# Delta rule and Hyena convolution on one core: scaled keys from ScalarE inside the inversion, a last level that updates one matrix, no barrier behind it, and the convolution's copies first

## What is computed

```python
a = jnp.where(strict, jnp.einsum('nbhid,nbhjd->nbhij', kb, kc) * decay, 0.0)
t_inv = lax.linalg.triangular_solve(eye + a, jnp.broadcast_to(eye, a.shape), left_side=True, lower=True)
u = t_inv @ (vc * bc[..., None])
w = t_inv @ (kb * jnp.exp(gc)[..., None])
k_dec = kc * jnp.exp(gc[..., -1:] - gc)[..., None]
...
v_new = u_i - jnp.einsum('bhck,bhkv->bhcv', w_i, state)
state = state * ge_i[..., None, None] + jnp.einsum('bhck,bhcv->bhkv', kd_i, v_new)
```

## Time and profile before

| | us |
|---|---|
| median of 3 runs | 2621.1 (2616.09, 2621.1, 2623.4) |
| the profiled execution | 2617.3 |
| its span | 2615.5 |
| PE busy | 2498.7 (96%) |
| DVE busy | 1501.8 (57%) |
| ACT busy | 938.6 (36%) |
| POOL busy | 835.9 (32%) |
| granted clock of PE, mean | 0.972 |

### The profile page before, as it was taken

How to read it: one execution, slowest core, us unless ns; L and a number is a source line. 1 busy time by engine, 2 the same in 40 slices (tenths; PEclk the granted TensorE clock), 3 DMA queues, 4 the chain that set the end, 5 groups by cost and what they waited for, 6 DMA issues and landing times.

```text
span 2615.5 us, 37266 instructions
## 1 busy us (share of the span) xinstructions
PE 2498.7 (96%) x14492; PEld 2053.0 (78%) x14492; DVE 1501.8 (57%) x2134; ACT 938.6 (36%) x1419; POOL 835.9 (32%) x446
## 2 busy tenths in 40 slices
PE   7899899999999989998999999999998999999998
PEld 5667887888888877866788888888886766788887
DVE  5766745635755878487555456654675477524242
ACT  4366213322223646336433222122255432433231
POOL 3433002454442222224223322322223331354443
PEclk9999888999997999999999999999998999999999
DMA  5412001444441110212013333422321020232222
GB/s 210 170 50 89 3 7 59 172 134 159 163 153 57 49 49 1 63 57 35 18 48 127 99 113 128 137 91 94 121 73 55 30 84 33 81 113 97 97 97 80
DMA packets 78567, 228.49 MB, mean 87 GB/s; under 512 B 21456, under 2 KB 23504, under 8 KB 77786
## 3 DMA queue, kind: packets, MB, share of 16 engines
q1 hardware_dynamic: 66216, 181.31, 20.9%
q10 hardware_dynamic: 12210, 45.20, 5.2%
HBM read 224.37 MB, written 2.12 MB: 87 GB/s over the span
## 4 chain that ended last, share of the span: by engine, by line
PE 83%; DVE 8%; ACT 4%; issue 4%; POOL 1%; DMA 1%; DVEq 0%; ACTq 0%; POOLq 0%; SPq 0%
PE ps L271 21%; PE ps L272 21%; PE ps L273 21%; PE ps L769 3%; PE ps L784 2%; PE ps L800 2%; PE ps L440 1%; PE ps L392 1%; POOL w_lo L2472 1%; DVE rstd L681 1%; PE ps L350 1%; PE ps L351 1%; PE ps L352 1%; DVE small L861 1%; PE ps L449 1%
## 5 line engine op out<-in xcount | busy, mean ns | idle before, releaser
L2472 POOL TENSOR_TENSOR w_lo<-ring,w_hi 128x1024 fp32r<-128x1024 f32 x292 | 711.5, 2437 | 1353.5 <-ACT w_hi L264 850.0
L271 PE MATMUL ps<-act_hi,w_hi 128*128 128x512 f32 x2280 | 840.9, 369 | 7.6 <-DVE mix_lo L957 6.0
L273 PE MATMUL ps<-act_hi,w_lo 128*128 128x512 f32 x2280 | 827.8, 363 | 0.0
L272 PE MATMUL ps<-act_lo_ffn,w_hi 128*128 128x512 f32 (+1 forms) x1408 | 512.9, 364 | 0.0
L271 PEld LDWEIGHTS ps<-act_hi,w_hi 128*128 128x128 f32 x2280 | 428.8, 188 | 91.1 <-issue 15.8
L273 PEld LDWEIGHTS ps<-act_hi,w_lo 128*128 128x128 f32 x2280 | 427.8, 188 | 71.5
L264 ACT CAST w_hi<-ring 128x1024 fp32r<-128x1024 f32 (+1 forms) x167 | 173.5, 1040 | 698.6 <-PE ps L273 610.8
L1150 ACT CAST w_hi<-ring 128x1024 fp32r<-128x1024 f32 (+1 forms) x132 | 137.5, 1043 | 460.9 <-PE ps L273 460.9
L272 PEld LDWEIGHTS ps<-act_lo_ffn,w_hi 128*128 128x128 f32 x1408 | 265.1, 188 | 42.2 <-issue 0.7
L1070 DVE SCALAR_TENSOR_TENSOR ada_place<-ada_place 128x1024 f32<-128x1024 f32 x164 | 252.4, 1539 | 23.6 <-DMA ada_place<-in_w_ada 9.8
L271 PE MATMUL ps<-hidden_hi,w_hi 128*128 128x512 f32 x704 | 256.3, 364 | 1.8 <-DVE hidden_lo L1231 1.5
(11 more groups left out here) (371 smaller groups left out, 3368.7 us busy)
## 6 DMA issues: line engine op xcount, KB each, us to landing
ring<-in_w_ffn SPq DMA_DIRECT2D x204, 512.0 KB, 3.3
ada_place<-in_w_ada ACTq DMA_DIRECT2D x82, 512.0 KB, 4.3
ring<-in_w_gdn SPq DMA_DIRECT2D x16, 512.0 KB, 3.3
mix<-in_w_ada SPq DMA_DIRECT2D x14, 512.0 KB, 3.5
ring<-in_w_hy SPq DMA_DIRECT2D x12, 512.0 KB, 3.3
ring<-in_w_dil_qk SPq DMA_DIRECT2D x8, 512.0 KB, 8.2
ring<-in_w_out SPq DMA_DIRECT2D x8, 512.0 KB, 3.2
ring<-in_w_diff_qk SPq DMA_DIRECT2D x8, 512.0 KB, 3.3
```

The source lines that it names most:

```text
L271: pe.matmul(out, w[0], x[0], start=start, stop=False)
L272: pe.matmul(out, w[0], x[1], start=False, stop=False)
L273: return pe.matmul(out, w[1], x[0], start=False, stop=stop)
L2472: pool.tensor_tensor(k.w_lo[:, a % SPLITS, :], k.ring[:, a % SLOTS, :], k.w_hi[:, a % SPLITS, :].bitcast(F32), ALU.subtract).then_inc(k.lo ...
```

## The change

- The scaled keys `kbe` and `k_tok` are made by ScalarE, in 32 ACTIVATEs of 128x128 that stand behind the copies of levels 0 to 3 of the inversion (one head per level).
- The last level leaves out the products and updates of `t`.
- The barrier behind the inversion is gone; the u products of a head wait for that head's `inv_updated`, the w products for `apply_kbe`.
- Apply's blocks are ordered u, u, w, w for two heads at a time. VectorE clears the state before it copies w.
- `keep_warm` at the end of apply is one matmul, not four.
- In Hyena, ScalarE's and VectorE's barrier behind the projection is gone, and all four `skipped` multiplications stand behind the copies of the bins and of z.

The diff, without the list of stages and with one of the engines' barrier lines for each of the two stages:

```diff
--- before.py
+++ after.py
@@ -1964,7 +1964,8 @@
         for h in range(GH):
             blk = slice(4 * h, 4 * h + 4)
             v.eng.wait_ge(k.sem("inv_z"), GH * lev + h + 1)
-            link(v, v.eng.tensor_tensor(m["t"][:, blk, :], m["t"][:, blk, :], small_bank(k, 4 + h), ALU.subtract))
+            if lev < LEVELS - 2:
+                link(v, v.eng.tensor_tensor(m["t"][:, blk, :], m["t"][:, blk, :], small_bank(k, 4 + h), ALU.subtract))
             v.eng.tensor_tensor(m["tt"][:, blk, :], m["tt"][:, blk, :], small_bank(k, h), ALU.subtract).then_inc(k.sem("inv_updated"), 1)
             v.eng.wait_ge(k.sem("inv_updated"), GH * lev + h + 1)
 
@@ -1989,33 +1990,44 @@
             for b in range(PAIRS):
                 i = 4 * h + b
                 for r in HALVES:
-                    pe.matmul(small_bank(k, 4 + h, r)[:, b, :], m["tt"][r, i, :], m["a"][r, i, :], start=True, stop=True)
+                    if lev < LEVELS - 2:
+                        pe.matmul(small_bank(k, 4 + h, r)[:, b, :], m["tt"][r, i, :], m["a"][r, i, :], start=True, stop=True)
                     last = pe.matmul(small_bank(k, h, r)[:, b, :], m["a"][r, i, :], m["tt"][r, i, :], start=True, stop=True)
             last.then_inc(k.sem("inv_z"), 1)
 
 
 def gdn_invert_scalar(k, s):
     m = gdn_views(k)
+
+    def keys(h):
+        for b in range(PAIRS):
+            i, at = 4 * h + b, GH * b + h
+            s.eng.activation(m["kbe"][:, i, :], m["k_tok"][:, i, :], ACT.Copy, scale=k.small[:, 80 + at:81 + at])\
+                .then_inc(k.sem("apply_kbe"), 1)
+        s.eng.wait_ge(k.sem("apply_kbe"), PAIRS * (h + 1))
+        for b in range(PAIRS):
+            i, at = 4 * h + b, GH * b + h
+            s.eng.activation(m["k_tok"][:, i, :], m["k_tok"][:, i, :], ACT.Copy, scale=k.small[:, 64 + at:65 + at])\
+                .then_inc(k.sem("apply_keys"), 1)
+
     for lev in range(LEVELS - 1):
         for h in range(GH):
             s.eng.wait_ge(k.sem("inv_x"), GH * lev + h + 1)
             s.eng.copy(m["a"][:, 4 * h:4 * h + 4, :], small_bank(k, h)).then_inc(k.sem("inv_x_kept"), 1)
             s.eng.wait_ge(k.sem("inv_x_kept"), GH * lev + h + 1)
+        if lev < GH:
+            keys(lev)
 
 
 def gdn_apply_vector(k, v):
     m = gdn_views(k)
     for h in range(GH):
-        blk = slice(4 * h, 4 * h + 4)
-        v.eng.tensor_tensor(m["kbe"][:, blk, :], m["k_tok"][:, blk, :], spread(by_head(k, 80)[:, h, :], P), ALU.mult).then_inc(k.sem("apply_kbe"), 1)
-        v.eng.wait_ge(k.sem("apply_kbe"), h + 1)
-        link(v, v.eng.tensor_tensor(m["k_tok"][:, blk, :], m["k_tok"][:, blk, :], spread(by_head(k, 64)[:, h, :], P), ALU.mult))
         link(v, v.eng.tensor_tensor(m["qkvg"][:, h, :], m["qkvg"][:, h, :], m["egc"][:, h, :], ALU.mult))
+    link(v, v.eng.memset(m["state"], 0.0))
     for n in range(2):
-        v.eng.wait_ge(k.sem("apply_made"), 2 * n + 2)
+        v.eng.wait_ge(k.sem("apply_turned"), n + 1)
         for e, r in enumerate(HALVES):
             link(v, v.eng.tensor_copy(m["wt"][:, 8 * n:8 * n + 8, r], k.bank(4 + 2 * n + e).rearrange("p (b n) -> p b n", b=8)))
-    link(v, v.eng.memset(m["state"], 0.0))
 
 
 def gdn_apply_scalar(k, s):
@@ -2024,25 +2036,31 @@
         s.eng.wait_ge(k.sem("apply_made"), h + 1)
         s.eng.copy(m["u"][:, 4 * h:4 * h + 4, :], k.bank(h).rearrange("p (b n) -> p b n", b=4)).then_inc(k.sem("apply_kept"), 1)
     s.eng.wait_ge(k.sem("apply_kept"), GH)
+    s.eng.wait_ge(k.sem("apply_keys"), GH * PAIRS)
 
 
 def gdn_apply_tensor(k, pe):
 
     m = gdn_views(k)
-    for h in range(GH):
-        pe.wait_ge(k.sem("apply_kbe"), h + 1)
-        for b in range(PAIRS):
-            i = 4 * h + b
-            for e, r in enumerate(HALVES):
-                pe.matmul(k.ps[r, h * 512 + b * P:h * 512 + (b + 1) * P], m["tt"][r, i, :], m["v_tok"][r, i, :], start=True, stop=True)
-        for b in range(PAIRS):
-            i = 4 * h + b
-            for e, r in enumerate(HALVES):
-                last = pe.matmul(k.bank(4 + 2 * (h // 2) + e, CHUNK, (i % 8) * CHUNK), m["kbe"][r, i, :], m["tt"][r, i, :],
-                                 start=True, stop=True)
-        last.then_inc(k.sem("apply_made"), 1)
+    for n in range(2):
+        for h in (2 * n, 2 * n + 1):
+            pe.wait_ge(k.sem("inv_updated"), GH * (LEVELS - 2) + h + 1)
+            for b in range(PAIRS):
+                i = 4 * h + b
+                for e, r in enumerate(HALVES):
+                    last = pe.matmul(k.ps[r, h * 512 + b * P:h * 512 + (b + 1) * P], m["tt"][r, i, :], m["v_tok"][r, i, :],
+                                     start=True, stop=True)
+            last.then_inc(k.sem("apply_made"), 1)
+        for h in (2 * n, 2 * n + 1):
+            pe.wait_ge(k.sem("apply_kbe"), PAIRS * (h + 1))
+            for b in range(PAIRS):
+                i = 4 * h + b
+                for e, r in enumerate(HALVES):
+                    last = pe.matmul(k.bank(4 + 2 * n + e, CHUNK, (i % 8) * CHUNK), m["kbe"][r, i, :], m["tt"][r, i, :],
+                                     start=True, stop=True)
+        last.then_inc(k.sem("apply_turned"), 1)
     pe.wait_ge(k.sem("apply_kept"), 1)
-    keep_warm(k, pe, 0, 4)
+    keep_warm(k, pe, 0, 1)
 
 
 def gdn_scan_tensor(k, pe):
@@ -2313,9 +2331,6 @@
         link(s, s.eng.copy(k.sq[:, 0, 0:S], k.bank(bank(0))))
         s.eng.copy(k.sq[:, 1, 0:S], k.bank(bank(2))).then_inc(k.sem(done), 1)
 
-    s.eng.wait_ge(k.sem("hy_taps_made"), 4)
-    for c in range(3):
-        skipped(c)
     s.eng.wait_ge(k.sem("hy_kernel_bins"), 1)
     s.eng.wait_ge(k.sem("hy_summed"), 1)
     left(0, odd_banks, "hy_kernel_left")
@@ -2324,7 +2339,9 @@
         s.eng.wait_ge(k.sem("hy_z_turned"), c + 1)
         s.eng.copy(b["z"][:, :, c * P:(c + 1) * P], k.bank(turned_bank(c)).rearrange("p (t n) -> p t n", t=4))\
             .then_inc(k.sem("hy_z_kept"), 1)
-    skipped(3)
+    s.eng.wait_ge(k.sem("hy_taps_made"), 4)
+    for c in range(4):
+        skipped(c)
     s.eng.wait_ge(k.sem("hy_bins"), 1)
     s.eng.wait_ge(k.sem("hy_kernel_kept"), 1)
     left(0, even_banks, "hy_bins_left")
@@ -2549,7 +2566,6 @@
     gdn_products_tensor(k, pe)
     k.after(pe, "gdn_products")
     gdn_invert_tensor(k, pe)
-    k.after(pe, "gdn_invert")
     gdn_apply_tensor(k, pe)
     k.after(pe, "gdn_apply")
     gdn_scan_tensor(k, pe)
@@ -2656,7 +2671,6 @@
     k.pairs["gqa"].scalar(s)
     end("gqa_attend")
     hy_project_scalar(k, s)
-    end("hy_project")
     hy_inverse_scalar(k, s)
     end("hy_inverse")
     along_scalar(k, s, "w_out_o", k.sem("mix_o_evac"), "mod_f1", k.x, S)
```

More of the change, by code:

```diff
@@ L79 @@
     "start", "norm1", "dil_project", "dil_attend", "gdn_project", "gdn_masks",
-    "gdn_products", "gdn_invert", "gdn_apply", "gdn_scan", "gdn_out", "mix1_split", "mix1_out", "mix1_post", "norm2",
+    "gdn_products", "gdn_apply", "gdn_scan", "gdn_out", "mix1_split", "mix1_out", "mix1_post", "norm2",
     "ffn1", "ffn1_post",
@@ L83 @@
     "mix_e_split", "mix_e_out", "mod_f0", "ffn2",
-    "mod_a1", "gqa_project", "gqa_attend", "hy_project", "hy_inverse", "mix_o_out", "mod_f1", "ffn3", "end",
+    "mod_a1", "gqa_project", "gqa_attend", "hy_inverse", "mix_o_out", "mod_f1", "ffn3", "end",
 ]
@@ L2614, in scalar_program @@
     gdn_invert_scalar(k, s)
-    end("gdn_invert")
     gdn_apply_scalar(k, s)
```

## The result

The changed kernel takes 2598.88 us (median of 4 runs, 2594.7 to 2601.37), the kernel before 2622.25 us (4 runs). The ratio is 0.9913, with a 95% interval of 0.9891 to 0.9935: 17 to 29 us less. The profiled execution has a span of 2596.8 us, 18.7 us less than before.

The account below looks back on a forecast made before the run. The prediction took TensorE, 83% of the chain that ended last, to bound the kernel. Gains of 1.89 + 2.05 + 7.6 + 4.45 = 16.0 us (delta rule) and 4.7 (Hyena), 20.7 together, from 2619.2 gave 2598.5 us, range 2591 to 2607.

Parts of the forecast that it names:

- Last level: Inversion's last level: half of the 128 second products go, taking 1.89 us from TensorE's path.
- No idle before apply: Between inversion and apply: u products wait only for their head's update, so TensorE's 2.05 us of idle go.
- ScalarE's keys: Inversion's first four levels: eight added ACTIVATEs each, 3.2 to 3.4 us, fit ScalarE's 3.86 us idle and cost nothing.
- seven of the eight multiplications: VectorE's lost key multiplications in apply: only the first was on the path, the other seven ran beside TensorE, worth nothing.
- Clock in apply: Apply: with no idle ahead the clock stays 1.00, so 15.2 us become 7.6, a gain of 7.6 us.
- the first rival: Apply's w products do not follow the clock: 2.9 us less gain, 2601.4 us; chance 0.08 together with late keys.
- End of apply: Last w block to scan: one warm matmul, VectorE's last copies decide, 1.85 us in place of 6.3, gain 4.45 us.
- Hyena: Hyena part: ScalarE's bins copy goes first, 3.3 us; shorter TensorE idle keeps the clock, 1.4 us more.
- The sum: Whole kernel: 16.0 us in the delta rule and 4.7 in Hyena, 20.7 us gained.
- The slower rival: Scan starts at half clock and never recovers: its 32 us become up to 64, total 2630 or 2638; chance 0.05.

Follow-up runs that it names:

- e11: The changed kernel with the barrier behind the inversion put back: 2600.61 us, ratio 0.9921.
- e7: The changed kernel with the scaled keys made by VectorE inside apply, no barrier: seven executions, one of 2604.24 us, six from 2626.42 to 2632.68.
- e9: The kernel of e7 run once more for a profile: 2629.88 us.
- e3: The kernel before with two warm matmuls added between the inversion and apply, filling TensorE's idle time: 2609.66 us, ratio 0.9972.
- e4: The changed kernel with one added wait, holding apply back until VectorE has cleared the state: 2606.09 us, ratio 0.9958.
- e6: The kernel before with apply's blocks in pairs, u, u, w, w, all else as before: 2610.39 us, ratio 0.9969.
- e5: The kernel of e4 (changed kernel, apply held back) with its blocks in the old order u, w, u, w: 2638.33 us, ratio 1.0072.
- e12: The changed kernel with no warm matmul at the end of apply: ten executions, four from 2598.74 to 2599.88 us, six from 2620.44 to 2625.78.
- e10: The kernel of e7 with four warm matmuls at the end of apply in place of one: 2604.8 us, ratio 0.9938.
- e8: The changed kernel with four warm matmuls at the end of apply in place of one: 2597.45 us, ratio 0.9918.

## Why the prediction was right

*Last level.* 1.9 us as summed (3.78 - 1.87). One sentence was wrong: VectorE's dropped updates were said to cost nothing either way. In the kernel before, the last head's `t` update, 0.42 us, ran from 308.50 us, inside TensorE's idle 2.05 us. The sum was not touched, since it counted that idle time whole.

*No idle before apply.* The u products start 3.8 us behind the last level's first record, before 7.8: 1.9 and 2.05 us as summed. With the barrier alone put back 0.65 us of idle return (e11). The rest of the 2.05 us is, by the rows of before, the first key on VectorE (309.60 to 310.44, 0.84 us) and the `t` update with its gap (0.46); no run put these two back one by one, so this part of the split is an estimate from the rows.

*ScalarE's keys.* Hidden, with 1.19 us left, and the levels start 5.72 us apart as before (297.34 to 303.06); 0.32 us each where the row of an exponential gave 0.395. The Trainium skill (ScalarE: Activation LUTs, Rules for kernel authors) gave an estimate of 0.41. What I undervalued was what they bring: I wrote that seven of the eight multiplications were worth nothing. That held for the sum, but with them on VectorE the scan starts 3.8 us later, and behind an idle time of 1.8 us; seven of the eight executions (e7, e9) were long.

*Clock in apply.* -7.7 us measured, -7.6 summed. The u blocks and the w blocks both double in speed (1.75 to 1.96 us for 32 records), so the first rival, w products held at the scan's 0.105 us, is out. e3 shows the cause, the idle time, by itself. But the change had a second way to the same gain, which the prediction did not see: with its order u, u, w, w the clock comes back inside apply even behind an idle time (e4, e6). In e4 apply takes 9.4 us in place of 15.2, so the greater part of the term is there although the idle time is long.

*End of apply.* 314.40 to 316.02 is 1.6 us where 1.85 were expected, before 6.3. TensorE idled 0.59 us of it, not about 1.

*Hyena.* 3.27 and 1.42 us against 3.3 and 1.4. The second was there in all ten profiles with this part of the change: behind the idle 1.30 us the 24 records took 10.57 us each time. But in six of the ten the later idle 2.36 us cost 1.7 us (8.83 us in place of 7.14), which the prediction had not looked at, so over many executions the part may be worth less than 4.7 us.

*The sum.* 20.7 us summed, 18.7 between the two profiled executions, 17 to 29 by the timed runs, 23.4 between their medians. That the forecast of 2598.5 us lies 0.4 us from the measured median is in part luck: it set out from 2619.2 us, and the median of before became 2622.25, so a start 3 us too low and a gain 2.7 us too small cancel. At both places the trace has the full terms: 16.3 and 4.7 us. The profiled execution of the changed kernel entered the inversion 1.7 us later (ScalarE's first copy at 278.32, before at 276.58), won 1.4 of it back in level 0, where the clock did not fall this time, and lost 1.9 us between the scan and Hyena; adding the half-clock time over stretches of 5 us gives 102 us there in both, so that loss is not the clock's, and its cause stays open. It is within the spread of the runs (2594.7 to 2601.37 us for the changed kernel).

*The slower rival* is real as a mechanism, and my argument against it was half right. A scan that is past its first step at full clock keeps it, in every profile; in e9 the first step began at full clock and lost it. But a cold one did not recover in any profile (59 us, e5 and e12), and I had called 1 us of idle safe because 2.05 us had cost the clock. The length of the idle time alone does not decide. Behind 1.64 us before the scan the clock was lost in most executions (e12), and behind 1.81 us it was kept in one (e7). The same idle 2.42 us in the inversion's level 0, which all fourteen profiles have, was followed by a fall in eleven and by none in three (the changed kernel, e3, e12). Behind 0.71 us between w blocks it fell in e7 and e9, and not in e10. The changed kernel has 0.59 us before the scan, and neither its profile nor any of its four times shows a cold scan; that it can never happen is not shown. The Trainium skill (TensorE: Matmul & The Clock Gate, What's actually happening) has the clock depend on how busy TensorE has been. By the profile's busy time the trace does not agree: at 10.00 of 10.00 us busy the clock stayed at 0.50 (e5). The runs show behind which products it came back: the second products of the inversion (to 0.96), the u blocks in pairs (e4, e6, e7, e9) and the four 128x512 warm matmuls (before). Under u and w in turn it did not come back in 15 us, and under the scan's products not in 59.

No version tried beats the changed kernel. That with four warm matmuls (e8) is as fast and leaves no idle time before the scan, so by these runs it is the safer one.

## What to carry to other kernels

Look at the granted clock behind each idle time of TensorE, and at how long it stays down: 2 us of waiting cost 7.7 us in apply here, and a scan that starts cold costs 27 us (59 in place of 32). Where a stage's products do not bring the clock back, fill the wait ahead of it, or put the work that does bring it back there first; when work is taken off another engine, ask whether it shortens a wait before such a stage. A kernel whose runs fall into two groups, as e12's at 2599 and 2624 us, may have a wait behind which the clock is lost in some executions only; profile one of each group. And when two versions are compared by one profile each, look at all such waits first, since a fall that came or stayed away by chance is worth 1.4 to 1.7 us here.

## What the runs showed of the hardware that was not expected

- The order of the same matmuls decides whether the clock returns: u, u, w, w at 0.57 and then 1.00 (e6), u, w, u, w at 0.50 for 15 us.
- TensorE can stay at 1.2 GHz through 75 us of unbroken matmuls (312 to 387 us, e5).
- The same program keeps or loses the scan's clock from one execution to the next: by their times 4 to 6 in e12, 1 to 7 in e7 and e9 together. The two that were profiled of this second program have nearly the same idle time before the scan, 1.81 us (kept) and 1.78 us (lost).
- An idle time of 2.42 us was followed by a fall of the clock in eleven profiles of fourteen, one of 2.36 us in six of fourteen, and one of 0.71 us in two of three (e7, e9, not e10).
